# A two-layer decoder step on one core: the ninth expert job uses the weights of the last pair, which TensorE scatters itself

## The reference

```python
def _hier_moe(u, rg_w, rg_b, re_w, re_b, w1, w3, w2):
    t = u.reshape(b_sz * seq_len, d)
    g_prob = jax.nn.softmax((t @ rg_w + rg_b).astype(F32), axis=-1)
    g_val, g_idx = lax.top_k(g_prob, 1)
    ...                                    # the four logits of that group
    e_val, e_idx = lax.top_k(e_prob, EXPERT_TOPK)            # 2 of 4
    weights = g_val * e_val / jnp.sum(e_val, axis=-1, keepdims=True)
    expert = g_idx * EXPERTS_PER_GROUP + e_idx
    combine = jnp.sum(jax.nn.one_hot(expert, N_EXPERTS, dtype=F32) * weights[..., None], axis=1)
    h1 = jnp.einsum('td,edf->tef', t, w1)                    # 16 experts, d = 1024, f = 512
    h3 = jnp.einsum('td,edf->tef', t, w3)
    act = jax.nn.silu(h1) * h3 * combine[:, :, None].astype(t.dtype)
    y = jnp.einsum('tef,efd->td', act, w2)
```

## Time and profile before

| | us |
|---|---|
| median of 3 runs | 1171.77 (1166.9, 1171.77, 1172.0) |
| the profiled execution's own time | 1167.13 |
| its span, first to last instruction | 1165.4 |
| PE busy | 1032.6 (89%) |
| DVE busy | 332.8 (29%) |
| ACT busy | 160.4 (14%) |
| mean granted TensorE clock | 0.928 of full |
| expert stage of layer 0, first W1 matmul to the last norm matmul | 426.4 to 720.0 |
| expert stage of layer 1, the same | 878.6 to 1156.7 |

### The profile page before, as it was taken

One profiled execution on the slowest core, in us unless ns is written; L12 is line 12 of the kernel. 1 busy time (PEld: TensorE's weight loads), 2 busy tenths in 40 slices (PEclk: granted clock), 3 DMA queues, 4 the chain that ended last, 5 costly groups with the idle time before them and its releaser, 6 DMA issues. The chain is left out here.

```text
span 1165.4 us, 12493 instructions
## 1 busy us (share of the span) xinstructions
PE 1032.6 (89%) x5312; PEld 577.3 (50%) x5312; DVE 332.8 (29%) x850; ACT 160.4 (14%) x300; POOL 40.9 (4%) x72
## 2 busy tenths in 40 slices
PE   5889999999879889999889848999979999988976
PEld 2556654673446554444444415777755444444424
DVE  1241134144423441111111116738461111101116
ACT  2200000022211210000000003045211010000012
POOL 0000000004100000000000010000000000000020
PEclk9899999977889979999999878999979999999988
DMA  9734677519962419999999990113726999999971
GB/s 387 296 134 175 260 287 288 217 46 334 419 267 94 195 41 412 421 421 421 420 421 421 421 370 5 72 73 146 293 73 268 407 421 420 421 420 421 421 283 45
DMA packets 47057, 330.84 MB, mean 284 GB/s; under 512 B 3634, under 2 KB 8642, under 8 KB 15506
## 3 DMA queue, kind: packets, MB, share of 16 engines
q1 hardware_dynamic: 33648, 299.12, 63.1%
q0 software_dynamic: 6672, 24.40, 5.6%
q10 hardware_dynamic: 6674, 6.44, 1.7%
HBM read 316.42 MB, written 13.52 MB: 283 GB/s over the span
## 5 line engine op out<-in xcount | busy, mean ns | idle before, releaser
L1328 PE MATMUL banks<-scr 128*64 128x512 f32 x512 | 123.2, 632 | 27.8 <-DMA scr<-in_ew 27.6
L745 PE MATMUL banks<-uT,ring 128*128 128x320 f32 x448 | 129.1, 449 | 9.9 <-DVE scr L1931 4.8
L1328 PE MATMUL banks<-ring,scr 128*64 128x512 f32 x512 | 114.7, 601 | 4.9 <-issue 4.9
L745 PEld LDWEIGHTS banks<-uT,ring 128*128 128x128 f32 x448 | 88.0, 198 | 51.9 <-issue 13.8
L1368 PE MATMUL banks<-ring,scr 128*64 128x512 f32 x512 | 113.4, 595 | 0.0
L1306 PEld LDWEIGHTS banks<-scr 128*128 128x128 f32 x864 | 103.2, 198 | 15.9 <-issue 13.2
L1306 PE MATMUL banks<-scr 128*128 128x128 f32 (+1 forms) x864 | 107.7, 284 | 2.5 <-DVE scr L1721 2.5
L1328 PEld LDWEIGHTS banks<-scr 128*64 128x64 f32 x512 | 38.1, 144 | 111.4 <-issue 67.0
L1328 PEld LDWEIGHTS banks<-ring,scr 128*64 128x64 f32 x512 | 37.5, 138 | 78.3 <-issue 74.3
L1368 PEld LDWEIGHTS banks<-ring,scr 128*64 128x64 f32 x512 | 35.3, 137 | 65.8 <-issue 64.0
L822 PE MATMUL banks<-ring,cT 128*32 128x512 f32 x384 | 54.0, 686 | 10.3 <-DMA ring<-in_w 10.3
(11 more groups left out here) (345 smaller groups left out, 991.0 us busy)
## 6 DMA issues: line engine op xcount, KB each, us to landing
ring<-in_ew SPq DMA_DIRECT2D x68, 2048.0 KB, 21.7
ring<-in_w SPq DMA_DIRECT2D x40, 2048.0 KB, 11.0
scr<-in_ew SPq DMA_DIRECT2D x34, 2048.0 KB, 24.8
yd<-scr POOLq DMA_DIRECT2D x16, 512.0 KB, 8.4
scr<-in_v POOLq DMA_DIRECT2D x16, 256.0 KB, 21.2
scr<-in_kT POOLq DMA_DIRECT2D x13, 256.0 KB, 10.6
out_hgrn<-scr ACTq DMA_DIRECT2D x4, 576.0 KB, 6.2
scr<-in_s POOLq DMA_DIRECT2D x1, 2048.0 KB, 10.4
```

The lines of the kernel that those rows point to most:

```text
L745: last = mm(out, a, b, start=(first and i == 0), stop=(final and i == len(pairs) - 1))
L1328: ins = mm(ps[bank][SLOTS * x:SLOTS * x + SLOTS, :], xe[:, kk, SLOTS * x:SLOTS * x + SLOTS], wab[SLOT[n]][:, x, kk % 4, :], start=(kk == 0 ...
```

## The change

- The 6 MB that the ninth job loaded are gone. DVE works out which expert is over 64 and swaps it with expert 14 in the order of experts (`order_i`), so that it stands first in the last pair; the ninth job then uses the last pair's six pieces. SP reads the experts of pairs 1 to 7 from `order_i` and waits for `over_ready` before pair 1. A surplus in expert 0 or 1 (whose weights are loaded before the routing is known) sends the stage to `dense`.
- Each piece, here and in the other stages, is loaded as two transfers of 1 MB.
- The ninth job is woven into the last pair: its tokens are gathered in the seventh job (`gather_most`), its W1 and W3 follow the last pair's, its W2 follows the last pair's W2.
- The last pair isn't stored: PE scatters it with a 128 x 320 matrix (`add_pair`). The two scatter matrices are turned in jobs 4 and 5 (`turn_back` after q = 3 and q = 4). The row fetch is issued after the seventh store.
- SP waits for the fetched rows before it loads the next stage's pieces.
- The sums run by pairs of chunks d and d+4, over seven PSUM banks. DVE adds the squares of chunks 1 to 5 in that order to those of chunk 0 (`add_square`), and PE sums three operands in place of eight. In layer 0 the multiplication by the gain follows after all eight chunks.
- PE runs matmuls whose result nobody reads (`idle`): 4 and 2 among and after the token transposes, 1 after the positions, 2 after the first gather.

The diff, cut to its core:

```diff
+            def experts(l, apart):
                 for p in range(NPAIR):
+                    if p == 0:
+                        pair = (0, 1)
+                    else:
+                        if p == 1:
+                            sp.wait_ge(sem("over_ready"), l + 1)
+                        pair = [bass.ds(sp.value_load(order_i[0:1, e:e + 1], min_val=0, max_val=NE - 1), 1)
+                                for e in (2 * p, 2 * p + 1)]
...
-                sp.wait_ge(sem("over_ready"), l + 1)
-                most = sp.value_load(most_i[0:1, l:l + 1], min_val=0, max_val=NE - 1)
-                for i in range(3):
-                    load(at + 6 * NPAIR + i, ...)
+            for t in range(TT):
+                sp.wait_ge(sem(f"rows_in{t}"), ROWS_BEFORE[t][0] + 32)
...
             def norm(n):
-                for m in range(DT):
+                for m in range(DT) if n == 0 else (0, DT - 2, DT - 1):
+                    if n >= 2 and m == 0:
+                        pe.wait_ge(sem(f"ye_evv{n // 2 - 1}"), NPAIR + 2)
...
+            def idle(n):
+                for _ in range(n):
+                    give(mm(ps[7][:, :], ident, const[:, 0:512], start=True, stop=True))
...
+            def gather_most(l):
+                pe.wait_ge(sem(f"pick_ready{l}"), NPAIR + 1)
+                for d in range(DT):
+                    for t in range(TT):
+                        ins = mm(ps[7][:, SLOTS * d:SLOTS * d + SLOTS], utok[:, t, P * d:P * d + P], pick[:, t, 0, :],
+                                  start=(t == 0), stop=(t == TT - 1))
...
+                def add_pair(d):
+                    if d == 0:
+                        pe.wait_ge(sem(f"ye_evv{l}"), NPAIR)
+                        pe.wait_ge(sem(f"ye_eva{l}"), NPAIR)
+                    c = P * (d % 4)
+                    give(mm(ps[SUM_BANK[d]][:, 0:T], ye[(NPAIR - 1) % 3][:, d // 4, c:c + P], back[0],
+                            start=False, stop=False))
...
+                for q in range(NPAIR):
+                    hidden(q, 0, 2, "h1_ps")
+                    hidden(q, 1, 3, "h3_ps")
+                    if q < NPAIR - 1:
                         gather(l, q + 1, 0)
+                        turn(q)
+                        gather(l, q + 1, 1)
+                        if q in BACK_AT:
+                            turn_back(BACK_AT.index(q))
+                        if q == NPAIR - 2:
+                            pe.wait_ge(sem(f"back_ev{l}"), 2)
+                            gather_most(l)
                     else:
                         hidden_most()
+                        turn(q)
+                    outputs(q)
+                outputs_most()
+                for d in range(3):
+                    for n in range(TT):
+                        turn_rows(d, (n,))
+                        turn_rows(d + 4, (n,))
+                    add_pair(d)
+                    add_pair(d + 4)
+                    add_most(d)
+                    add_most(d + 4)
...
+            def add_square(l, i, chain, more=1):
+                v.wait_ge(sem("sq_ready"), DT * (2 * l + 2) + i + 1)
+                ins = tt(sq[:, 0, :], sq[:, 0, :], sq[:, i, :], ADD)
...
+                step(tt(change, swaps[:, :, h:h + 1].broadcast_to([P, 2 * TT + 1, NE]), swaps[:, :, 0:NE], SUB))
+                step(tt(change, change, over(swap, 2 * TT + 1, 1), MUL))
+                v.tensor_reduce(total.unsqueeze(2), change, AX, ADD)
+                step(tt(swaps[:, :, 0:NE], swaps[:, :, 0:NE], change, ADD))
+                step(tt(swaps[:, :, h:h + 1], swaps[:, :, h:h + 1], total.unsqueeze(2), SUB))
+                step(cp(order_i[0:1, :], swaps[0:1, 2 * TT, 0:NE]))
```

More of the change, by code:

```diff
@@ L421, in expert_rows @@
             def expert_rows(l):
[L423 removed]
+                for q in range(NPAIR - 1):
                     pool.wait_ge(sem(f"ye_evv{l}"), q + 1)
@@ L1264, in dense @@
                         pair(p, it)
-                for i in range(3):
-                    while gone:
-                        give(mm(ps[7][:, 0:1], ones[:, :], ones[:, 0:1], start=True, stop=True))
-                    piece(AT_MOE[l] + 6 * NPAIR + i)
-                    used(AT_MOE[l] + 6 * NPAIR + i)
                 while gone:
@@ L1353, in turn, with turn_most @@
                         give(ins, f"actT_ps{l}" if f == FT - 1 else None)
+                def turn_most():
+                    pe.wait_ge(sem(f"act_in{l}"), NPAIR + 1)
+                    for f in range(FT):
+                        ins = pe.transpose(ps[1][:, PAIR * f:PAIR * f + PAIR], sg_most[:, P * f:P * f + P], ident)
+                        give(ins, f"actT_ps{l}" if f == FT - 1 else None)
                 def outputs(q):
@@ L1427, in routed @@
-                turn_back()
-                while gone:
-                    give(mm(ps[7][:, 0:1], ones[:, :], ones[:, 0:1], start=True, stop=True))
-                pe.wait_ge(sem(f"ye_eva{l}"), NPAIR)
-                for d in range(4):
-                    turn_rows(d)
-                for d in range(4):
-                    add_most(d)
-                for d in range(4, DT):
-                    pe.wait_ge(sem(f"out_ev{l}"), d - 3)
-                    turn_rows(d)
+                        turn(q)
@@ L1773, in experts @@
+                    if l == 1:
+                        gained(4, i)
+                    if 2 <= i < DT - 1:
+                        add_square(l, i - 1, link)
+                if l == 0:
+                    for i in range(DT):
+                        gained(2, i)
             def experts(l):
```

311 lines of the change are left out of this document (177 added, 134 removed).

## The result

| | before | after |
|---|---|---|
| first measurement: median, lowest to highest | 1171.88 (1166.9 to 1178.6), 4 runs | 1118.85 (1114.54 to 1121.7), 4 runs |
| ratio, 95% interval | | 0.9541 (0.948 to 0.9601) |
| second measurement, with e5 | 1175.23 (1160.4 to 1187.06), 11 runs | 1115.48 (1108.61 to 1128.74), 6 runs |
| ratio, 95% interval | | 0.9512 (0.9455 to 0.957) |
| profiled execution, its span | 1167.13, 1165.4 | 1121.7, 1119.6 |

What follows compares the result with a forecast made beforehand. The weight stream bounds the pairs, the DRAM round trip the stage ends. Span 1165.4 - 31.6 - 18.9 - 3 - 2 + 0.7 = 1110.6 us, execution 1112.3, forecast 1113; own range 1103 to 1121, with rivals 1102 to 1130.

Steps and rivals of the forecast that it cites:

- The bound and the place of the gain: Expert stages: weight stream bounds the pairs; the change pays in end gaps of 40 us and some 27 us.
- The eighth job, step by step: Last pair: inserted gather partly absorbed by W3's load stall of 2.3 and 2.6 us; W3 to sums 26.3 us.
- Rows not last: End of layer 0's expert stage: fetched rows ready at 667 to 678, PE at 671; low side taken.
- The sums: Scatter sums at the stage end: 1.75 us a chunk, 14.0 for eight, against 12.6 before.
- DVE in layer 1: Layer 1's sums: first chunk ready after 3.0 us, DVE's chain then 12.7; ACT's root 18.9 us earlier.
- The routing: Before the experts: idle matmuls hold the clock up, saving 3 us in layer 0 and 2 in layer 1.
- clock 1.00 from the transposes to W1: Sign that the forecast is right: full PE clock through the routing up to the first W1.
- The loads: Pieces cut in two and SP's order reads: 0 to 2 us on the whole, 0.7 taken.
- rival 4: Half-size transfers stream worse in pairs 1 to 7: 1197 us at 1 us more a piece; chance 0.02.
- rows last: Fetched rows arrive after PE is ready for the sums: 7 us a layer, 1127 us; chance 0.10.
- Only bytes pay: Stage ends: dropping six pieces gives 30 us, added PE work eats the round trip's gain: 1137 us; chance 0.05.
- Idle matmuls at the low clock: Routing: idle matmuls run at 1.2 GHz, +8 us a layer in place of -5 in all: 1134 us; chance 0.07.

Runs made afterwards that it cites:

- e5: The changed kernel run again unchanged, as a control: 1115.48 us, ratio 0.9512 to the kernel before.
- e4: The changed kernel with the last pair stored too and the row fetch issued behind that eighth store: 1155.26 us, ratio 0.9901 to the kernel before.
- e12: The changed kernel with SP no longer waiting for the fetched rows before loading the next pieces: 1119.86 us in one run.
- e9: The changed kernel with layer 1's multiplication by the gains only behind the whole scatter, as in layer 0: 1118.31 us in one run.
- e11: The changed kernel without DVE's additions of squares; PE sums all eight chunks' squares: 1115.64 us in one run.
- e7: The changed kernel without any of its idle (filler) matmuls: 1125.05 us, ratio 0.9589 to the kernel before.
- e10: The changed kernel without the two filler matmuls behind the routing's last gather: 1122.22 us in one run.
- e2: The kernel before with every piece loaded as two transfers of 1 MB: 1175.51 us, ratio 1.0117 to the kernel before.
- e1: The changed kernel with pieces of w, outside the expert stages, loaded whole as 2 MB transfers: 1110.49 us, ratio 0.952 to the kernel before.
- e6: The changed kernel with whole pieces of w, layer 1's gains behind the whole scatter, and no filler behind the last gather: 1112.8 us, ratio 0.9503.
- e3: The kernel before without the ninth job's 6 MB reload, that job using the last pair's pieces: 1152.6 us, ratio 0.9885 to the kernel before.

## Why the prediction was right, and where it was off

*The bound and the place of the gain* were right. The end of the two stages gave 48.1 of the 50.5 us forecast for them.

*The eighth job, step by step*: 26.3 us forecast from W3 to the sums, 26.5 measured (648.27 to 674.78). From W1 to the first sum 244.6 and 242.3 forecast, 244.4 and 242.6 measured. The absorbed stall was seen as predicted.

*Rows not last*: right, the low side was the true one; e4 and e12 show the cover. The first fetch waited 7.8 us for the store, not 10.3.

*The sums*: 14.0 forecast (14.2 by its own terms, 0.81 + 0.57 + 0.4 a chunk); eight chunks took 14.4 in layer 0 (674.78 to 689.18), at 3.35 for two and 2.14 to 2.2 for each of the last two, which stand alone. `add_most` side by side or in turn is 0.81 - 0.07 for two chunks, 0.37 a chunk, near the 0.4 taken. In layer 0 the norm's step came 18.1 us after the first sum, forecast 18.0.

*DVE in layer 1* is the first mis-sized term. I had 3.0 us to the first chunk and 12.7 for the chain (12.9 by 8 x 1.33 and 5 x 0.45). It was 3.5 (1091.81 to 1095.26) and 14.0, since a chunk with gain and `add_square` takes 1.86 and not 1.78, and DVE stood idle for 0.59 us before the third chunk. With 0.7 us of a low clock in the ones-matmul, absent in e5, that makes 2.5 us: -16.4 in place of -18.9. e9 and e11 confirm that DVE is what is last.

*The routing*: 5 us forecast, 3.9 measured up to W1. In layer 0 the mechanism, the filler holding the clock at 2.4 GHz, is shown by e7. The gather starts 1.5 us earlier (1.4 forecast) and is 1.7 shorter (1.6), and behind it 0.9 is put back (1.8 at most). The forecast also counted up to 1.7 us of a shorter first W1. It came, 7.09 in place of 8.78, but it lies behind W1's start, and how much of it reaches the sums the runs don't tell. In layer 1 the filler held the clock only up to the gather:

```profile
839.33 7.07 PE L1340 MATMUL banks<-scr 128*128 128x128 f32 x48 [0.25 <-DVE scr L1812]
```

The same gather took 5.62 in layer 0. So "clock 1.00 from the transposes to W1" was right for layer 0 and wrong for layer 1, in e5 as well (7.22), though PE had paused there for no more than 0.82 us since the first transpose. Why the clock fell stays open. W1 does not start when the filler ends: 2.1 and 1.1 us of idle time stand there, and e10 shows that without the filler W1 comes no sooner. The Trainium skill ("TensorE: Matmul & The Clock Gate", Part 4: PE-mode transpose) has it that transposes don't count as work. e7 doesn't test it: the clock falls among the second transposes, but behind 4.36 us in which PE stood idle.

*The loads* are the second mis-sized term, and the step whose reason failed. I put 0.7 us on the halved pieces because a stretch with 256 KB loads streamed at 419 GB/s. The rate did stay: 421 to 423 in the pairs, which refutes rival 4. But the rate of the sum wasn't the question ahead of the expert stage, where two queues share it. There w comes later when it is halved, and PE waits longer for it: 7.9 to 12.0 us between 200 and 390 in the nine profiles with halved w, against 3.8 to 4.5 in the five with whole pieces. What that does to T is less sure. T lay at 399.4 to 408.0 in the eight profiles of the changed kernel and its variants with halved w, and at 390.8 to 401.8 in the five with whole pieces, a mean of 404.3 against 396.4. But e2, the halving alone, has 396.8, within the 391.9 to 401.8 of the kernel before. And among the five, T goes with the clock granted between 270 and 345 (0.92 and 0.91 where it is 390.8 and 391.9, 0.84 to 0.87 in the rest), and that differs for one and the same program. So the longer waits are shown, and that they are the 6.2 us is likely and not shown. Whether halved w costs the whole kernel time, e1's and e6's medians leave open: they lie 3 to 8 us lower, inside the intervals.

*The rivals*: rows last, refuted. Only bytes pay, refuted by e3, which gives 13 to 19 of 53 us. Idle matmuls at the low clock, refuted: the first eight records take 3.60 us in both layers, at the full clock. The change does what it says.

The four misses, 5.5 us ahead of the stage, 1.1 in the routing, 2.5 in layer 1 and -0.1 in layer 0, add up to the 9.0 us between the forecast span of 1110.6 and 1119.6.

## What to carry to other kernels

When a stage ends in a store and a gather of what was just computed, price the round trip itself: here it was two thirds to four fifths of the gain, and the 6 MB per layer that went with it a quarter to a third. Let the last unit of work stay on the chip and the round trip run beside it. Before calling a cut of transfers free, look at whether another queue streams at the same time, since the total rate doesn't show whose data comes later. And where an engine is given a job in place of another (squares on DVE), add up its steps per chunk against the pace of its feeder in each layer apart.

## What the runs showed of the hardware

- With w as rows of half the length, in transfers of 1 MB, loads of 256 KB on POOL's queue landed in 12.6 and 7.3 us, and with whole pieces in 20.7 and 10.3.
- A store of 512 KB was seen 10.3 and 8.4 us after its issue where the reload of weights streamed beside it (427 and 340 GB/s in all), and 3.1 to 3.2 us after it in e3 and e4, where it didn't (159 and 164).
- Matmuls on data that nobody reads paid for themselves: with 8.5 us of them in a routing the clock was 1.00 and not 0.73 in layer 0, 0.92 and not 0.73 in layer 1, and the routing 2.7 and 2.4 us shorter.
- The same program scatters by 9 to 10 us in the start of its expert stage (before 391.9 and 401.8, after 399.4 and 408.0), while the expert stage itself repeats within 0.3 us before and 2.1 after. A difference of some us ahead of a stage isn't to be read from one pair of profiles.
